# Squares of the norms added by GpSimd, routing of the second block's experts from unnormed rows, and another start and end of the program

## The reference

```
def rms_norm(x, w):
    y = x * lax.rsqrt(jnp.mean(x * x, axis=-1, keepdims=True) + EPS)
    return y * w
for layer in range(DEPTH):                     # DEPTH = 2
    h = rms_norm(x, norm_mix[layer]);  x = x + hybrid_mixer(h, ...)
    h = rms_norm(x, norm_ffn[layer])
    x = x + (swiglu(h, ...) if layer % 2 == 0 else moe_swiglu(h, ...))
x = rms_norm(x, final_norm)
# moe_swiglu: logits = t @ router_w; top_vals, top_idx = top_k(logits, 2)
#   gates from softmax(top_vals); out += gates[:, e] * ((silu(t @ w1[e]) * (t @ w3[e])) @ w2[e])
for i in range(4):                             # second block
    x = x + mixer_i(rmsnorm(x, norm_mix[i]));  x = x + swiglu_2(rmsnorm(x, norm_ffn[i]), ...)
```

## Time and profile before

| what | value |
|---|---|
| median of 3 runs | 3052.69 us (3052.58 to 3054.29) |
| profiled execution, its own time | 3051.69 us |
| its span, first to last instruction | 3049.9 us |
| mean granted TensorE clock | 0.984 |
| busy PE / DVE / ACT / POOL | 2972.4 / 2030.6 / 1632.7 / 249.4 us |

### The profile page before, as it was taken

The page is one execution under the profiler, slowest core; times in us unless marked ns, Lnnn a source line. Parts: engine busy times, 40 slices in busy tenths (PEclk is TensorE's granted clock), DMA queues, the critical chain, the costliest instruction groups (busy, mean ns, idle before and its releaser), DMA issues.

```text
span 3049.9 us, 46933 instructions
## 1 busy us (share of the span) xinstructions
PE 2972.4 (97%) x20370; PEld 2725.7 (89%) x20370; DVE 2030.6 (67%) x1817; ACT 1632.7 (54%) x1611; POOL 249.4 (8%) x199
## 2 busy tenths in 40 slices
PE   8999999999989999999999899999899999999999
PEld 7999999999978888888788497999799999786999
DVE  5787665688758888888788565554555455565553
ACT  5446444535557767767676462445644454353442
POOL 0130110023000000000000202100001010012010
PEclk9999999999989999999999899999999999999999
DMA  6444555544449989989899050556155555431453
GB/s 214 160 143 154 177 179 171 184 148 149 156 161 371 349 344 361 367 336 351 341 377 363 16 166 28 176 177 228 48 174 177 183 180 177 141 112 55 140 185 119
DMA packets 358819, 613.15 MB, mean 201 GB/s; under 512 B 11375, under 2 KB 323397, under 8 KB 323536
## 3 DMA queue, kind: packets, MB, share of 16 engines
q1 hardware_dynamic: 354592, 597.73, 56.3%
q10 hardware_dynamic: 3536, 12.23, 1.2%
q0 software_dynamic: 480, 0.12, 0.0%
HBM read 608.99 MB, written 1.05 MB: 200 GB/s over the span
## 4 chain that ended last, share of the span: by engine, by line
PE 94%; ACT 3%; DVE 2%; issue 1%; DMA 1%; ACTq 0%; POOLq 0%; POOL 0%; DVEq 0%
PE ps L327 18%; PE ps L329 18%; PE ps L328 18%; PE ps L1191 5%; PE ps L1193 5%; PE ps L1192 5%; PE ps L1172 3%; PE ps L1170 3%; PE ps L1171 3%; PE ps L1670 2%; PE ps L628 2%; PE ps L1685 2%; PE ps L1640 2%; PE ps L354 1%; PE ps L1626 1%; PE ps L1240 1%
## 5 line engine op out<-in xcount | busy, mean ns | idle before, releaser
L271 DVE TENSOR_TENSOR wlo<-raw,whi 128x2048 fp32r<-128x2048 f32 (+1 forms) x573 | 1314.0, 2299 | 609.2 <-ACT whi L260 605.2
L260 ACT ACTIVATE whi<-raw 128x2048 fp32r<-128x2048 f32 (+1 forms) x573 | 1083.7, 1894 | 276.3 <-PE ps L329 145.0
L327 PE MATMUL ps<-HX,whi 128*128 128x256 f32 x1808 | 519.2, 287 | 10.4 <-DVE wlo L271 5.6
L329 PE MATMUL ps<-HX,wlo 128*128 128x256 f32 x1808 | 513.4, 284 | 0.0
L328 PE MATMUL ps<-HX,whi 128*128 128x256 f32 x1808 | 513.3, 284 | 0.0
L327 PE MATMUL ps<-HXB,whi 128*128 128x256 f32 x1760 | 500.3, 284 | 0.0
L329 PE MATMUL ps<-HXB,wlo 128*128 128x256 f32 x1760 | 498.1, 283 | 0.0
L328 PE MATMUL ps<-HXB,whi 128*128 128x256 f32 x1760 | 498.1, 283 | 0.0
L327 PEld LDWEIGHTS ps<-HX,whi 128*128 128x128 f32 x1808 | 349.0, 193 | 13.6 <-ACT whi L260 6.1
L328 PEld LDWEIGHTS ps<-HX,whi 128*128 128x128 f32 x1808 | 349.0, 193 | 0.9 <-issue 0.5
L329 PEld LDWEIGHTS ps<-HX,wlo 128*128 128x128 f32 x1808 | 348.7, 193 | 0.0
(11 more groups left out here) (317 smaller groups left out, 4355.7 us busy)
## 6 DMA issues: line engine op xcount, KB each, us to landing
raw<-in_c_experts SPq DMA_DIRECT2D x264, 1024.0 KB, 4.9
raw<-in_w_in SPq DMA_DIRECT2D x72, 1024.0 KB, 5.0
raw<-in_ff_w_gate SPq DMA_DIRECT2D x44, 1024.0 KB, 5.3
raw<-in_ff_w_up SPq DMA_DIRECT2D x44, 1024.0 KB, 5.3
raw<-in_ff_w_down SPq DMA_DIRECT2D x32, 1024.0 KB, 5.1
raw<-in_dense_w SPq DMA_DIRECT2D x30, 1024.0 KB, 5.3
raw<-in_hy_w_in SPq DMA_DIRECT2D x24, 1024.0 KB, 5.1
raw<-in_ff_w_down SPq DMA_DIRECT2D x16, 768.0 KB, 4.7
```

Of the source, the lines that this page charges most:

```text
L260: e.activation(m.whi[:, i % NSPLIT, 0:n], m.raw[:, i % NRAW, 0:n], ACT.Copy).then_inc(*k.up("act", "hi", i))
L271: e.tensor_tensor(m.wlo[:, i % NRAW, 0:n], m.raw[:, i % NRAW, 0:n], hi, ALU.subtract).then_inc(*k.up("dve", "lo", i))
L327: e.matmul(o, wh, xh, start=first and t == k0, stop=False)
L329: i = e.matmul(o, wl, xh, start=False, stop=final and t == k1 - 1)
```

## The change

It has five parts.

1. **Sums by GpSimd.** `pool_sums` adds the squares of tiles 2, 4 and 6 (two tiles at once, 128 x 512) onto those of tiles 0 and 1, and the second half onto the first (128 x 256). PE is left with one matmul of ones, in `pe_last_sums`, at the place of the last pair. For the norms hgrn1 and ffn3 GpSimd adds tiles 0 to 5 and PE takes 6 and 7 itself (three matmuls). The norms moe and final are as before.
2. **Start.** X is loaded in two halves on SP, the constants move from ACT's queue to SP's behind the first six panels, the first panel of f comes as two half panels of 4 row blocks, and ACT and DVE do four tiles of HX, then a half panel, and again; the squares come behind them. An Exp on one value stands ahead of the wait for X.
3. **Routing from unnormed rows.** In stage out of hgrn1, ACT and DVE write X times gain to buffer 7 (`routed_rows`), and PE multiplies them with the router's weights as stationary operand (L671, out 8 x 256) in three pairs between panels and one behind. The result is turned to rows of tokens, and the maxima are taken of it. The turned rows get rs as they leave PSUM (`m.rst`), and the difference of the two maxima gets it before the Exp.
4. **Order in the expert stage.** DVE does maxima, ranks and places first, then the low parts of the rows, then the gates (`dve_gated`). `pool_rows` multiplies buffer 7 by rs on GpSimd (four times 128 x 512); only the branch for overfull experts reads it.
5. **End.** X is written in four transfers: tiles 0 to 3, 4 and 5, 6, 7.

```diff
-def pe_last_sums(e, k, m, s):
-    pe_sums(e, k, m, s, 6, 2)
-    k.release("sum", s)
+def pe_last_sums(e, k, m, s, whole=True):
+    o = pe_take(e, k, m, "sum", s)
+    e.wait_ge(*k.at("sq sum", s))
+    i = e.matmul(o[:, 0:L], m.ones[:, :], m.sq[:, 0, :], start=True, stop=whole)
+    for c in () if whole else (6, 7):
+        e.wait_ge(*k.at("sq", s, c))
+        i = e.matmul(o[:, 0:L], m.ones[:, :], m.sq[:, c, :], start=False, stop=c == 7)
+    i.then_inc(*k.up("mm", "sums", s))
+def pool_sums(e, k, m, s, whole=True):
+    q = m.buf(11)
+    for c in (2, 4, 6) if whole else (2, 4):
+        e.wait_ge(*k.at("sq", s, c + 1))
+        e.tensor_tensor(q[:, 0:2 * L], q[:, 0:2 * L], q[:, c * L:(c + 2) * L], ALU.add).then_inc(*k.up("pool"))
+        e.wait_ge(*k.own("pool"))
+    e.tensor_tensor(q[:, 0:L], q[:, 0:L], q[:, L:2 * L], ALU.add).then_inc(*k.up("pool", "sq sum", s))
...
-    pe_gemm(e, k, m, s, "out", m.HX, range(4), fresh=("mx", s),
-            after=lambda j: pe_sums(e, k, m, s, 2 * j - 2, 2) if j else None)
+    if l == 1:
+        pe_hold(e, k, m, "route", s)
+    pe_gemm(e, k, m, s, "out", m.HX, range(4), fresh=("mx", s), after=lambda j: pe_route(e, k, m, s, 2 * j - 2) if l and j else None)
+def pe_route(e, k, m, s, c0):
+    o = ps(k, m, "route", s)
+    e.wait_ge(*k.at("router"))
+    for c in (c0, c0 + 1):
+        e.wait_ge(*k.at("xg", s, c))
+        i = e.matmul(o[0:8, 0:L], moe_views(m)["rw"][:, c, :], routed_rows(m, c)[0], start=c == 0, stop=c == 7)
...
+def act_begin(e, k, m, a, panels):
...
+    for half in range(2):
+        for c in range(4 * half, 4 * half + 4):
+            e.wait_ge(*k.at("x", "x", c))
+            e.activation(m.HX[:, 0, c, :], m.X[:, c, :], ACT.Copy, scale=m.col("norm_mix", c)).then_inc(*k.up("act", "xh", "x", c))
+        act_feed(e, k, m, panels)
...
+def pool_rows(e, k, m, s, last):
+    e.wait_ge(*k.at("ht", s, 1, 1))
+    e.wait_ge(*k.at("rstd", last))
+    for j in range(4):
+        x = m.buf(7)[:, j * 512:j * 512 + 512].rearrange("p (a n) -> p a n", a=2)
+        e.tensor_tensor(x, x, m.wide_rs, ALU.mult).then_inc(*k.up("pool"))
...
 def sp_end(e, k, m, out, last):
+    for c0, c1 in ((0, 4), (4, 6), (6, 7), (7, 8)):
+        for c in range(c0, c1):
+            e.wait_ge(*k.at("x", last, c))
+        e.dma_start(out[:, c0:c1, :], m.X[:, c0:c1, :]).then_inc(*k.land("out_done", "out"))
```

More of the change, by code:

```diff
@@ L212, in panel_list @@
     hgrn(0)
+    first = a["w_in"][0][:, 1024:1280]
+    out[0:1] = [[(0, 4, 256, kview(first, 0, 256, 4 * h, 4 * h + 4))] for h in range(2)]
     ffn(a["dense_w1"][0], a["dense_w3"][0], a["dense_w2"][0])
@@ L502, in pool_begin, with dve_begin @@
     e.memset(m.epst[:, :], EPS).then_inc(*k.up("pool", "ones"))
[L505 to L512, removed]
+def dve_begin(e, k, m, panels):
     lo = m.par[:, COLS["lower_bounds"]:COLS["lower_bounds"] + 16]
@@ L520, in dve_begin @@
     e.tensor_tensor(e1, l1, mx, ALU.subtract).then_inc(*k.up("dve", "lb less"))
+    for half in range(2):
+        dve_ahead(e, k, m, "x", 4 * half, 4, (m.HX, lambda c: m.col("norm_mix", c)))
+        dve_feed(e, k, m, panels)
     e.wait_ge(*k.at("lb exp"))
@@ L655, in act_hgrn @@
         act_panel(e, k, m, panels)
+        if l == 0 and j == 0:
+            act_panel(e, k, m, panels)
         if j == 0:
@@ L925, in pool_hgrn, with pe_ffn @@
             pool_times_norm(e, k, m, s, name, j, x, "normed", s, name, j)
-def pe_ffn(e, k, m, s, last, after=None, sums=True):
+def pe_ffn(e, k, m, s, last, after=None):
     for j in range(11):
@@ L1417, in dve_places, with dve_gated @@
     if p:
+        e.wait_ge(*k.at("ga", s, p - 1, 7))
+    e.wait_ge(*k.own("dve"))
+    for i in range(2):
+        for j in range(2):
+            rc = v["rk"][:, j, 2 * p + i:2 * p + i + 1]
+            e.tensor_scalar(m.SELR[:, j, i, :], v["iota"], rc, None, ALU.is_equal).then_inc(*k.up("dve", "places", s, p))
+def dve_gated(e, k, m, v, s, p):
+    if p:
         e.wait_ge(*k.at("sgt", s, p - 1))
@@ L1705, in pe_hyena @@
     pe_back(e, k, m, s, 1, 1)
-    pe_hold(e, k, m, "sum", s)
-    pe_gemm(e, k, m, s, "out", m.HX, range(4), fresh=("zx", s),
-            after=lambda j: pe_sums(e, k, m, s, 2 * j - 2, 2) if j else None)
+    pe_gemm(e, k, m, s, "out", m.HX, range(4), fresh=("zx", s))
 def act_absolute(e, k, m, s, o_):
@@ L2060, in pe_attn @@
     back(3)
-    pe_hold(e, k, m, "sum", s)
-    pe_gemm(e, k, m, s, "out", m.HX, range(4), fresh=("ax", s),
-            after=lambda j: pe_sums(e, k, m, s, 2 * j - 2, 2) if j else None)
+    pe_gemm(e, k, m, s, "out", m.HX, range(4), fresh=("ax", s))
 def act_attn(e, k, m, a, panels, s, last, nxt):
@@ L2392, in pool_program @@
     pool_hyena(e, k, m, "hy0", "final")
+    pool_sums(e, k, m, "hy0")
     pool_ffn(e, k, m, "ffn1")
+    pool_sums(e, k, m, "ffn1")
+    pool_sums(e, k, m, "attn")
     pool_ffn(e, k, m, "ffn2")
+    pool_sums(e, k, m, "ffn2")
+    pool_sums(e, k, m, "pool")
     pool_backward(e, k, m, "hy1")
     pool_ffn(e, k, m, "ffn3")
+    pool_sums(e, k, m, "ffn3", False)
     pool_hyena(e, k, m, "hy1", "ffn3")
+    pool_sums(e, k, m, "hy1")
     pool_ffn(e, k, m, "ffn4")
@@ L2498, in pe_program @@
     pe_sums(e, k, m, "final", 0, 8)
+    k.release("sum", "final")
     pe_hyena(e, k, m, "hy0", "final")
```

193 lines of the change are left out of this document (115 added, 78 removed).

## The result

The changed kernel takes 3014.47 us (median of 4 runs, 3012.10 to 3015.02), the kernel before 3053.49 (4 runs, 3052.58 to 3055.47): a ratio of 0.987, 95% interval 0.9853 to 0.9887. The profiled execution took 3014.79 with a span of 3013.0, that is 36.9 less than the span before, at a granted clock of 0.986 on the mean. By the medians the change saves 39.0 us; what follows is read from the traces, which differ by 36.9.

The account below looks back on a forecast made before the run. PE was taken to bound the kernel (busy 2972.4 of 3049.9 us). Savings of 20.4 + 2.2 + 1.6 + 6.7 + 7.5 + 1.6 = 40.0 us from 3051.69 gave 3011.7, as a median 3012.7, range 3004 to 3026.

Parts of the forecast that it names:

- the passages: From stage out to a SwiGLU, four times: PE would wait 0.2 us each for DVE's low parts, 0.8 in all.
- Sums off PE: Norms' matmuls of ones between panels: seven norms save 21.2 us, 20.4 after waits for low parts; ffn3 saves 2.2.
- GpSimd and DVE collide: Two-SBUF-input DVE operations and reading GpSimd ones exclude each other; 4.5 us taken in routing, from nothing to 5.3.
- stage pool: Norm sums between short matmuls: saves 1.6 us, the middle between 0.3 (both adds collide) and 2.9 (neither).
- Routing: From the squares' wait to the experts: logits 12.2 us earlier, gather 6.7 us earlier, bounds 5 and 11.
- Start: Kernel start: first matmul at 9.6, second panel at 20.1 instead of 28.64; 7.5 us taken, bounds 5 and 9.5.
- The slow stretch that I allowed for: At the start: PE's pause for GpSimd might bring a second 1.2 GHz stretch of 6.8 us, costing 3.4.
- End: Final write of X: an eighth of the bytes left for the last transfer saves 1.6 us, bounds 1.0 and 2.3.
- Undisturbed: Rival, 15%: DVE escapes GpSimd's products in routing and the sum for x is in time; 3006.
- The lost race: Rival, 18%: GpSimd's last add stands behind DVE, PE waits 1.7 us at each of seven norms; 3025 to 3037.
- Waits that take PE's saved time: Rival, 4%: PE's saved time returns as waits for weights or DVE; 3040 to 3052.
- Slower: Rival, 3%: 42 adds and 4 products on GpSimd each hold up DVE and PE, 60 us less the 40; 3072.

Follow-up runs that it names:

- e3: Changed kernel without GpSimd's adds of squares (it zeroes one column and signals), so PE sums one tile's squares in eight only; 3010.60 us, ratio 0.9856.
- e1: Changed kernel with DVE's order turned round in stage out of hgrn0, hgrn1 and attn: add to X and HXB low parts before the weight panel's; 3021.79 us.
- e4: Changed kernel with the sums of squares of nine norms (all but x, hgrn1, moe, final) back on PE as matmul pairs; 3033.17 us, ratio 0.9934.
- e6: Changed kernel with ACT's squares in stage out of hgrn0, attn, hy0 and hy1 moved behind the next panel's rounding; 3013.15 us, ratio 0.9867.
- e2: Changed kernel with `pool_rows` on GpSimd waiting for the last low part of the turned rows instead of starting when rs is ready; 3011.63 us, ratio 0.9863.
- e7: Changed kernel with DVE's small work on `lower_bounds` moved behind the low parts of the first whole panels; 3016.03 us, ratio 0.9874.
- e8: Changed kernel with X written by one transfer at the end, as before the change; 3017.01 us, ratio 0.988.

## Why the prediction was right, point by point

The time lies in the range and 1.8 us from the forecast; what the two traces differ by is 3.1 less than the forecast's 40.0. That the number came so near is partly luck: the passages cost 4.7 more than forecast, start and end gave back 1.4 that was not forecast, and by the medians the saving is 39.0 where the traces have 36.9.

**Sums off PE: right by the matmul, wrong at the passages.** A panel takes 5.76 instead of 6.62, so 0.86 for a pair, the one matmul left costs 0.44, and PE never waits for GpSimd at it. The step that failed is the sentence "PE would want the last at about 343.6, so 0.2 each, 0.8 in all". Four such norms without a cost at the passage would save 12.1; they saved 6.6. The cost was 5.5, not 0.8, and the 4.7 between them are more than the whole error of the sum. I moved PE's first panel by the one pair behind the last panel and left DVE's times of the earlier trace rows where they were. But three pairs go ahead of it too, and DVE's loop of 6.19 us, hidden behind PE's 6.62 before, can't follow at 5.76. e3 excludes GpSimd, e1, e4 and e6 show the loop from three sides.

**GpSimd and DVE collide: right, the size within its bounds.** In DVE's second pass three operations, not four, were held up ahead of msk, since the first (L1411) began at 852.14, ahead of GpSimd's 852.33: 2.9 us, forecast 4.5; the range was nothing to 5.3. In stage pool it cost 1.5 of the 2.6 it could, so 1.7 saved, as forecast (1.6). At the start it is there as well (1.1), and I didn't look for it among operations of 8 columns. One sentence of that step doesn't hold in general: "the waiting one goes next". In e1 the waiting add stood behind two low parts in a row.

The Trainium skill, page "SBUF — State Buffer", section "Who interferes with whom", says that `tensor_scalar` can contend with GpSimd as well. I had written that no row shows it; e2 does, with L1449 at 1.05 us instead of 0.17 beside GpSimd's products, and the reciprocal behind it at 0.17.

**Routing: the sum right, two terms off against each other.** Logits copied 4.5 us behind the first wait (forecast 4.6), gather at 17.0 (18.2 by the steps of the sum), so 7.9 ahead of the old 24.9 instead of 6.7. Against that: the three routing pairs between panels were taken at nothing, and two of them show 0.29 each more than the sums' pairs they replace; from the gather's start to the experts' it took 0.24 more; and 0.6 was lost again between the first expert and hy0.

**Start: the time right, its cause not.** 20.31 for the second panel where 20.1 was forecast, but what is waited for is the low part, not the sum. The first matmul was 0.8 late (10.41) because the first half panel was rounded at 9.05, not 8.3. The slow stretch that I allowed for didn't come in this execution, where PE had waited 1.13 us; it came in e7 and e8 behind waits of 1.95 and 1.82, with a granted clock of 0.50 for 3.4 us from 20.1 and 20.2, and cost them 1.6 and 1.5. e8's start is the changed kernel's own, so this is a matter of the execution too.

**End: 2.1 instead of 1.6**, since the last transfer lands 1.9 us behind its issue, where I had taken 2.3 (3.9 less 1.6).

**The rivals.** Undisturbed: no, the collision is there. The lost race: not in this kernel, but one other order of DVE's work brings it about (e1), so it was close by. Waits that take PE's saved time: 5.5 + 0.6 us of it, far from all. The reason that I gave against it doesn't hold, though: DMA shares are not below 0.95 where it matters, they are 1.10 in the earlier trace rows and 0.98 from 1480 to 1500 us of the kernel before, and there the wait for weights grew from 3.51 to 3.80 us. Slower: 46 operations of GpSimd cost 2.9 + 1.5 + 1.1 = 5.5 us, not 60.

## What to carry to other kernels

When work is taken off the engine that bounds, work out the period of every other engine's loop for one panel and compare it with the new period of the bound, not only the one step at the border: a loop that was 7% faster than PE became 7% slower. And when adds go to GpSimd, look at which operations of DVE with two SBUF inputs, however small, stand beside them on a path that is waited for: four products that only the branch for overfull experts reads cost 2.9 us because they were free to begin in the middle of such a chain, and one wait moved them.

## What the runs showed of the hardware that I had not expected

- The cost of meeting GpSimd doesn't depend on DVE's size: 128 x 8 or 128 x 16 values take 0.7 to 1.3 us instead of 0.17, until GpSimd's operation ends. Operations with one SBUF input (TENSOR_REDUCE, RECIPROCAL) or with one from PSUM (L967) pass at 0.17, 0.20 and 0.68. A TENSOR_SCALAR with one input does not always pass (L1449 in e2).
- GpSimd can be kept out over two operations of DVE: 5.50 us for an add of 1.30 (e1), though it got in after one in e7 (2.65 instead of 0.73) and in the earlier trace rows.
- Two executions of one kernel, with the same waits up to there, differed by 1.06 us in one gather of 32 matmuls: the granted clock was at its lower level (1.2 GHz) from 855.2 to 868.9 us in one and from 852.7 to 866.4 in the other.
- The same wait at hgrn0 was followed by a slow stretch in one execution and not in another: 1.72 us in e3 with one of 3.4 us behind it, 1.74 in the changed kernel with none.
